# Forgetting attention on one core: the scalar engine's third value round goes ahead of an item's exponentials, and its first key round ahead of the keys' split

## The reference, cut to what matters

```python
q_a, k_a, v_a, f_a, ... = split(rmsnorm(h) @ w_in)
c = cumsum(log_sigmoid(f_a + b_forget), axis=1)
s = einsum('bqhd,bkhd->bhqk', q_blk, k_all) * dh ** -0.5
s = where(mask, s + c_q - c_k, -inf)                    # causal, per frame
p = softmax(s, axis=-1)
o = einsum('bhqk,bkhd->bqhd', p, v_all)
```

## Time and profile before

| | |
|---|---|
| median of 3 runs | 1681.83 us (1680.42 to 1682.17) |
| the profiled execution | 1680.76 us |
| its span, first to last instruction | 1679.0 us |
| PE busy | 1651.5 us, 98% |
| DVE busy | 1083.5 us, 65% |
| ACT busy | 775.8 us, 46% |
| POOL busy | 310.2 us, 18% |
| mean granted clock of PE | 0.999 |

### The profile page before, as it was taken

How to read it: one execution, slowest core, us unless ns; L and a number is a source line. 1 busy time by engine, 2 the same in 40 slices (tenths; PEclk the granted TensorE clock), 3 DMA queues, 4 the chain that set the end, 5 groups by cost and what they waited for, 6 DMA issues and landing times.

```text
span 1679.0 us, 27411 instructions
## 1 busy us (share of the span) xinstructions
PE 1651.5 (98%) x9540; PEld 1489.3 (89%) x9540; DVE 1083.5 (65%) x2322; ACT 775.8 (46%) x1630; POOL 310.2 (18%) x438
## 2 busy tenths in 40 slices
PE   8999999999999999999999999999999999999998
PEld 8999999999999988989988899888888888888886
DVE  7556666553999744454445597888877667774744
ACT  6477777765777533352233333222222334443521
POOL 1311111115333211124532230000000000000242
PEclk9999999999999999999999999999999999999999
DMA  5221212231222554563443422444432763444641
GB/s 187 77 61 41 79 47 59 67 110 36 74 57 67 163 179 160 160 210 123 147 140 111 134 85 94 131 144 144 144 131 105 258 220 111 132 149 125 192 163 75
DMA packets 164314, 205.34 MB, mean 122 GB/s; under 512 B 16152, under 2 KB 113240, under 8 KB 164208
## 3 DMA queue, kind: packets, MB, share of 16 engines
q1 hardware_dynamic: 164208, 203.97, 38.0%
HBM read 144.85 MB, written 57.28 MB: 120 GB/s over the span
## 4 chain that ended last, share of the span: by engine, by line
PE 80%; DVE 9%; ACT 4%; issue 4%; POOL 2%; DMA 0%; DVEq 0%; ACTq 0%; SPq 0%; POOLq 0%
PE gb L503 8%; PE gb L3173 6%; PE gb L2290 5%; PE sc L3173 5%; PE gb L2825 4%; PE gb L2661 4%; PE sc L2825 4%; PE tp L3173 4%; PE tp L2825 4%; PE tp L798 3%; PE sc L2449 3%; PE tp L2449 3%; PE gb L930 3%; PE gb L931 2%; PE gb L932 2%
## 5 line engine op out<-in xcount | busy, mean ns | idle before, releaser
L930 PE MATMUL gb<-Xh,wh 128*128 128x384 f32 (+1 forms) x504 | 175.9, 349 | 0.0
L489 POOL TENSOR_TENSOR wl<-raw,wh 128x256 fp32r<-128x256 f32 x168 | 125.0, 775 | 264.2 <-ACT wh L474 175.4
L931 PE MATMUL gb<-Xh,wl 128*128 128x384 f32 (+1 forms) x504 | 170.7, 339 | 0.0
L932 PE MATMUL gb<-Xl,wh 128*128 128x384 f32 (+1 forms) x504 | 170.7, 339 | 0.0
L3297 POOL TENSOR_TENSOR wl<-raw,wh 128x1024 fp32r<-128x1024 f32 x2 | 5.3, 2626 | 559.0 <-ACT wh L3288 559.0
L503 PE MATMUL gb<-Xh,wh 128*128 128x384 f32 (+1 forms) x288 | 103.9, 361 | 0.0
L503 PE MATMUL gb<-Xh,wl 128*128 128x384 f32 (+1 forms) x288 | 97.4, 338 | 0.0
L503 PE MATMUL gb<-Xl,wh 128*128 128x384 f32 (+1 forms) x288 | 97.3, 338 | 0.0
L930 PEld LDWEIGHTS gb<-Xh,wh 128*128 128x128 f32 x504 | 95.0, 189 | 0.1
L931 PEld LDWEIGHTS gb<-Xh,wl 128*128 128x128 f32 x504 | 95.0, 188 | 0.0
L932 PEld LDWEIGHTS gb<-Xl,wh 128*128 128x128 f32 x504 | 94.8, 188 | 0.0
(11 more groups left out here) (548 smaller groups left out, 4777.4 us busy)
## 6 DMA issues: line engine op xcount, KB each, us to landing
zr<-u_scr SPq DMA_DIRECT2D x91, 256.0 KB, 3.0
raw<-in_w_in SPq DMA_DIRECT2D x70, 256.0 KB, 3.2
u_scr<-ustore SPq DMA_DIRECT2D x26, 576.0 KB, 3.6
u_scr<-ustore SPq DMA_DIRECT2D x13, 768.0 KB, 3.2
sig_scr<-sig SPq DMA_DIRECT2D x16, 576.0 KB, 3.1
raw<-in_w_up SPq DMA_DIRECT2D x36, 256.0 KB, 4.4
kc<-in_cache_fox_k SPq DMA_DIRECT2D x8, 1024.0 KB, 5.6
vc<-in_cache_fox_v SPq DMA_DIRECT2D x8, 1024.0 KB, 7.6
```

Source lines behind the costliest of these rows:

```text
L489: nc.gpsimd.tensor_tensor(wl[U.slot][:, q], raw[U.slot][:, q], wh[U.slot][:, q].bitcast(F32), ALU.subtract).then_inc(w_lo if x == 3 else w ...
L930: nc.tensor.matmul(gb[c][:, 0:x1 - x0], wh[U.slot][:, ws], Xh3[:, k, x0:x1], start=(k == 0), stop=False)
L931: nc.tensor.matmul(gb[c][:, 0:x1 - x0], wl[U.slot][:, ws], Xh3[:, k, x0:x1], start=False, stop=False)
L932: last = nc.tensor.matmul(gb[c][:, 0:x1 - x0], wh[U.slot][:, ws], Xl3[:, k, x0:x1], start=False, stop=(k == KT - 1))
```

## The change

Two moves in `fox_act`. At t = 4 ACT reads the third value round before the exponentials of the step's item, where it was read after them. At t = 5 it copies the key round to `tm` before it splits the next head's keys, where the split came first. Each place occurs four times, once for each pair of heads. The key rounds at t = 6 and 7 and the split at t = 13 meet nothing that they could change places with. Nothing is added or removed.

```diff
                 for m, x in FOX_HI[s]:
                     hi_half(act, Unit(m), x)
+                if p < 4 and t == 4:
+                    v_round_act(act, p, t - 2)
                 if s < ITEMS:
                     fox_exp_act(act, s)
-                if s % 8 == 5 and (s + 3) // 8 < 8:
-                    k_split_act(act, (s + 3) // 8)
-                if p < 4 and t in (2, 3, 4):
+                if p < 4 and t in (2, 3):
                     v_round_act(act, p, t - 2)
                 if p < 4 and t in (5, 6, 7):
                     k_round_act(act, p, t - 5)
+                if s % 8 == 5 and (s + 3) // 8 < 8:
+                    k_split_act(act, (s + 3) // 8)
                 if s % 4 in (1, 2) and (s + 3) // 4 < 16:
                     q_split_act(act, (s + 3) // 4, s % 4 - 1)
```

## The result

The changed kernel takes 1683.85 us at the median of 20 runs (1681.97 to 1684.91) against 1681.26 us of the kernel before, run beside it (20 runs, 1679.93 to 1682.39). The ratio is 1.0014, with a 95% interval of 1.0008 to 1.0021: 1.3 to 3.5 us slower. The medians differ by 2.6 us. The loss is real, and smaller than the 0.2% that I had set as the limit of "no change". That limit was too wide: with 20 runs of each, a loss of 0.14% stands clear of the interval. The forecast of 1684.4 us stood on the first median, 1681.83; on the median of these runs it would have been 1683.9.

The account below looks back on a forecast made before the run. PE, busy 98% of the span, was taken to bound the kernel. The value move's -1.4 us and the key move's +4.0 make +2.6: 1683.4 us from the profiled 1680.76, 1684.4 on the median; range 1680.0 to 1686.8.

Parts of the forecast that it names:

- The first move: T(3,1), t = 4: V(2) read before the exponentials removes PE's pause, 0.38 us a pair, 1.4 us over four pairs gained.
- Rival B: T(5,1) behind K(1)'s copy: key move costs in full, value move brings nothing; 1685.8 us, up to 1688.5; chance 0.24.
- The second move: t = 5, K(0)'s copy ahead of the keys' split: T(5,1) comes 0.97 us later on the third pair, 4.0 us in all.
- the 0.06 us that T(4,1) was to gain: K(0)'s copy on ACT would start at 245.68 instead of 245.74, bringing T(4,1) forward 0.06 us, 0.2 us over four pairs.
- The split was late: ACT at t = 5: the keys' split would start at 246.30 instead of 244.63, 1.67 us late.
- the two that hold the scaling: Item 5's scaling on ACT: DVE's reciprocal would release it at 248.84, ACT's own queue already at 248.56.
- The scaling was 1.40 us late: Item 5's scaling on ACT would start at 248.84 instead of 247.53, 1.31 us late.
- some 0.6: K(1) on PE would lose some 0.6 us because DVE frees T(4,0) about 0.8 us late, without adding to the cost.
- The idle time of 0.34 us: ACT's idle time ahead of K(1)'s copy, third pair, would absorb 0.34 of 1.31 us, leaving that copy 0.97 us late.
- A: Slack in DVE or ACT before K(1) hides the split's lateness; only gains stay, -1.6 us, 1680.2 us; chance 0.14.
- C: Pauses at T(3,1) and T(4,1) both go, -3.8 us, 1678.0 us; chance 0.03.
- D: PE's clock falls to 1.2 GHz at the longer pauses among the transposes, costing 20 us; chance 0.01.

Follow-up runs that it names:

- the last version: Kernel before plus value round's move, K(0)'s transposes sooner on PE, odd heads' split away from t = 5, reciprocal ahead of split at t = 13: 1676.91 us, 0.9976.

## Why the prediction was right

**The sum.** -1.4 and +4.0 gave +2.6 us; the medians give +2.6. The single runs of each move give -1.6 and +3.7. Over the four pairs the trace of the changed kernel gives -1.27 us for T(3,0) to the scores (0.19, 0.36, 0.35, 0.37) and +3.75 us for T(4,0) to T(5,1) (1.01, 0.91, 0.93, 0.90). Both terms were a little large, in opposite directions. That the sum met the difference of the medians to a tenth is luck: the interval of that difference is 1.3 to 3.5 us, and the distances add up to +2.5.

**The first move.** V(2) was read at once, the pause went, and the later exponentials cost nothing: the reciprocal of item 4 even came 0.55 us sooner after V(2)'s transposes (1.99 us, before 2.54). Rival B had the gain vanish; the run of that move alone excludes it at the edge of its interval, that of the same move with K(0) sooner on PE does so again, and the distances exclude it outright.

**The second move, point by point.** K(0)'s copy started 0.69 us after its transposes. The working had 0.64, taken from K(1), but K(0)'s had been 0.70 in the kernel before, so the 0.06 us that T(4,1) was to gain did not come: its pause is 0.31 us in both. The split was late by 1.74 us against T(4,0), where I had 1.67. The reciprocal was the later of the two that hold the scaling, as said, and by 0.44 us where the working had 0.28. The scaling was 1.40 us late, against 1.31. K(1) lost 0.63 us, against "some 0.6", and it did not add. The one link mis-sized in a way that counted is the last: K(1)'s copy began 1.04 us after the start of item 6's exponentials, when it no longer waited for PE. The idle time of 0.34 us that I took off is counted from the ends in the profile, 1.15 us after that start, and ACT's instructions overlap a little. The two errors, +0.09 and -0.11, nearly cancelled, and the cost came out at 0.93 us a pair for 0.97.

**The rivals.** A, that the lateness is hidden, falls with the key round's move alone, +3.7 us. C, that T(4,1)'s pause goes, falls with the changed kernel and with the split moved away: the pause stayed at 0.31 us. It needed PE's earlier transposes as well. D, the clock: the mean granted clock of the changed kernel was 0.998, the level of 2.4 GHz, and 1.00 from 60 to 390 us, where the weight load paused for up to 0.9 us at the transposes. No run went to 1.2 GHz, so none shows the 20 us that D would have cost. What the Trainium skill says in "TensorE: Matmul & The Clock Gate", part 4, of transposes and the clock gate had no effect to be seen here, where the transposes stand among matmuls.

## What to carry to other kernels

When an engine waits for a copy, look at what the copy itself was waiting for: if its input is finished only some time after its turn comes (here 1.1 us), giving it an earlier turn moves nothing but the instructions behind it, and every one of them is late by the wait. Two causes that end at the same moment have to be removed together, as the last version did with the transposes and the split. A long instruction without a near deadline (here the keys' split, needed three steps later) belongs where its engine idles, and a short one that others wait for (the reciprocal) goes ahead of it; look at the first round of a loop by itself, since its idle times are others.

## What I had not expected

At t = 13, where nothing had been changed, ACT waited 0.97 us for a reciprocal that stood behind the split's low part, and PE lost some 0.16 us by it at each of the three places. The split at t = 1 cost the first pair 1.2 us and the other three nothing. And the part of the kernel from K(2) of the last pair to the end, which no edit touches, varied between the ten profiled executions by 1.7 us (1346.6 to 1348.3): with the value round's move alone K(2) came 1.6 us sooner, and the span was only 0.8 us shorter. For moves of this size the distance between two instructions tells more than a span.
